# The second block's norm totals in a two-block transformer kernel: from 16 matmuls over feature tiles to two sums on VectorE and four matmuls

## The chip, the cores and the metric

The kernel runs on one core of one Trainium2 chip. The metric is the device time of one execution in microseconds (us).

## The reference, cut to what matters

Two transformer blocks run one after the other on 256 tokens of 1024 features, in float32. The first ends with a norm of its own, and the second begins with a norm, so two stand in a row:

```python
def rmsnorm(x, g):
    y = x * rsqrt(mean(x * x, axis=-1) + EPS)
    return y * g
x1 = rmsnorm(x0, norm_final_g)       # end of the first block
hn = rmsnorm(x1, attn_norm_g_2)      # start of the second
proj = hn @ w_in_2                   # split into xc, b_gate, c_gate, q, k, v
```

Behind it come a short convolution, differential attention, a projection, and a mixture of 32 experts, whose weights (96 units of 2 MB) are all read from memory.

Both norms need one number a token. The first needs the total of x0 squared over the features. The second needs the mean of x1 squared, which is the first's factor squared times the total of (x0 g) squared. So the kernel makes two totals from x0, a plain one and one weighted by g squared, and the products of both norms are applied later: `proj` is computed from x0 times the two gains, and the factors of the tokens (`rstd`, `r12`) come in where q, k and v are normed or copied out.

## The kernel before, in words

**Layout.** The residual `xT` is stored with features on the 128 partitions, in KD = 8 feature tiles of 256 tokens. Every dense matmul is made in three: weights and activations are split into a high part (rounded to fp32r) and a low part (the rest), and high x high, low x high and high x low are summed. The weights of an item (`q2`, `k2`, `v2`, ...) come in four chunks of two feature tiles. ScalarE writes the high part of a chunk (`split`, L570 to L580), VectorE subtracts to get the low part (`split`, L1647 to L1654), TensorE multiplies (`chunk`, L1002 to L1033). There are four buffers for chunks; ScalarE's split of a chunk waits until TensorE has used the chunk four before it. A chunk of q2 or k2 is 12 matmuls of 512 columns.

**Order.** Each engine's program is written out by hand, and so is the order of work. Semaphores join them. SP issues the loads in the order of a list; a load waits until the last item in its slot was split by VectorE (L448) and, for experts, until the unit ten before it was used by TensorE (L479).

**The edited stage** begins when the first block's last residual is there, tile after tile.

- ScalarE (L803 to L814): for each of the 8 tiles it writes the high part of the input and a square of `xT` into `n_sq` (`norm_square`, L588 to L594); then it splits q2's chunks 2 and 3, all of k2, two chunks of v2; then it waits for the spreads (`norm_bc` at 4), copies the second one out (L812), squares q2 (L814) and splits the rest of v2.
- TensorE (L1313 to L1326): q2's chunks 0 to 2; the totals (`norm_totals`, L1077 to L1086: for each tile and each half of the tokens one matmul of 128 x 128 squares with the two columns of `gain_sq`, 1 and g squared, into PSUM); q2's chunk 3; k2's chunks 0 and 1; two spreads (`norm_spread`, L1088 to L1094), which put `rstd` and `r12_sq` of each token into every partition; k2's chunks 2 and 3; then v2, which waits for q2 to be copied out.
- VectorE (L2066 to L2133): low parts of the input, splits of q2's last two chunks and k2's first; the wait for the totals (`norm_sum` at 3) and the mean; one split of k2; then a chain of small steps with POOL, which computes the powers (L535, L544), to `r12_sq` (L2081); copies of q2 (L2086); k2's last two splits; the wait for the spreads; eight scalings of `xT` (L2092); the sum of q2's squares (L2109); v2's four splits.

`gain_sq` is filled at the start by VectorE (L1717, L1722). `n_t` is the second half of `wb`, `n_sq` the first; `wc` is scratch space.

Of the kernel before, what the change touches and what calls it, by code (L numbers as in the profile page):

```python
# [15 lines left out]
P = 128  # L16
# [177 lines left out]
def build(nc, t, out):  # L194
# [8 lines left out]
    def S(name):  # L203
        if name not in sems:
            sems[name] = ctx.enter_context(nc.semaphore(name))
        return sems[name]

    def sb(name, shape, dt=F32):
        return ctx.enter_context(nc.sbuf_tensor(name, shape, dt))

    with ctx:
# [34 lines left out]
        scale_m = sb("scale_m", [P, KD])  # L246
        scale_f = sb("scale_f", [P, KD])
        scale_2 = sb("scale_2", [P, KD])
        gain_sq = sb("gain_sq", [P, KD, 2])
        r12 = sb("r12", [P, TT])  # L250
        r12_sq = sb("r12_sq", [P, TT])
        eps_r = sb("eps_r", [P, TT])
# [36 lines left out]
        n_sq = wb[:, 0:KD * SEQ].rearrange("p (k n) -> p k n", k=KD)  # L289
        n_t = wb[:, KD * SEQ:2 * KD * SEQ].rearrange("p (k n) -> p k n", k=KD)  # L290
        n_row = wc[:, 1152:1152 + SEQ]
        CKQ = Q_RANK + KV_RANK + ROPE
        cqkv = wc[:, 0:TT * CKQ].rearrange("p (t n) -> p t n", t=TT)
        fqT = wa[:, 0:1024].rearrange("p (m n) -> p m n", m=4)
# [267 lines left out]
        def _(act):  # L562
# [7 lines left out]
            def split(name, a=0, b=None):  # L570

                it = IT[name]
                for ci in range(a, len(it["chunks"]) if b is None else b):
                    c = it["c0"] + ci
                    if ci == 0:
                        act.wait_ge(S(f"slot{it['slot']}_loaded"), it["loaded"])
                    if c >= CHUNKS:
                        act.wait_ge(S("chunk_used"), c - CHUNKS + 1)
                    src, n = raw_chunk(it, ci)
                    nc.scalar.activation(wh[:, c % CHUNKS, 0:n], src, ACT.Copy).then_inc(S("chunk_high"), 1)  # L580
# [225 lines left out]
                nc.scalar.activation(hH[:, k, :], xT[:, k, :], ACT.Copy, scale=scale_2[:, k:k + 1]).then_inc(S("norm_high"), 1)  # L806
                norm_square(2, k, XT_BASE[2] + k + 1)
            split("q2", 2)
            split("k2")
            split("v2", 0, 2)  # L810
            act.wait_ge(S("norm_bc"), 4)
            nc.scalar.activation(r12_sq_b, ps[:, 5, 0:SEQ], ACT.Copy).then_inc(S("r12_out"), 1)  # L812
# [185 lines left out]
        def _(pe):  # L998
            def mm(o_, l, r, start, stop):
                return nc.tensor.matmul(o_, l, r, start=start, stop=stop, skip_group_check=True)  # L1000
# [70 lines left out]
            def ada_turn(n):  # L1071
# [2 lines left out]
                    ins = nc.tensor.transpose(ps[:, 6, s * P:s * P + P], ada_row[:, s * P:s * P + P], ident[:])  # L1074
                ins.then_inc(S("ada_turned"), 1)

            def norm_totals(n, bank, k0=0, k1=KD):  # L1077

                rows_n = 2 if n == 2 else 1
                for k in range(k0, k1):  # L1080
                    pe.wait_ge(S("norm_sq"), SQ_BASE[n] + k + 1)
                    for tt in range(TT):
                        ins = mm(ps[:, bank, rows_n * tt:rows_n * tt + rows_n], n_sq[:, k, tt * P:tt * P + P],
                                 gain_sq[:, k, :] if n == 2 else ones[:, 0:1], k == 0 and tt == 0, k == KD - 1)
                if k1 == KD:
                    ins.then_inc(S("norm_sum"), 1)  # L1086

            def norm_spread(ready, count, src, bank, c0=0):  # L1088

                pe.wait_ge(S(ready), count)  # L1090
                for tt in range(TT):
                    ins = mm(ps[:, bank, c0 + tt * P:c0 + tt * P + P], src[:, tt:tt + 1].to_broadcast([P, P]), ident[:],
                             c0 == 0 and tt == 0, True)
                ins.then_inc(S("norm_bc"), 1)  # L1094
# [219 lines left out]
            chunk("q2", 0, hH, hL, True, ready=in_2)  # L1314
            chunk("q2", 1, hH, hL, True, ready=in_2)
            chunk("q2", 2, hH, hL, True, ready=in_2)
            norm_totals(2, 6)
            chunk("q2", 3, hH, hL, True, ready=in_2)
            chunk("k2", 0, hH, hL, True)
            chunk("k2", 1, hH, hL, True)  # L1320
            norm_spread("norm_rstd", 3, rstd, 7)
            norm_spread("norm_r12", 1, r12_sq, 5)
            chunk("k2", 2, hH, hL, True)
            chunk("k2", 3, hH, hL, True)
            pe.wait_ge(S("q2_out"), 2)
            linear("v2", hH, hL, True)  # L1326
# [311 lines left out]
        def _(dve):  # L1638
# [21 lines left out]
            def mean_sq(dst, src, width, sem):  # L1660
                V.tensor_scalar(dst, src, 1.0 / width, EPS, ALU.mult, ALU.add).then_inc(S(sem), 1)

            def norm_mean(n, count, bank):

                rows_n = 2 if n == 2 else 1
                dve.wait_ge(S("norm_sum"), count)
                cols = ps[:, bank, 0:rows_n * TT].rearrange("p (t r) -> p r t", t=TT)
                mean_sq(ms[:, 0:TT], cols[:, 0, :], D, "norm_ms")
                return cols

            def norm_apply(n, bc, scale, shift, between=None):

# [37 lines left out]
            for part in two_pi_parts():  # L1710
# [3 lines left out]
            V.tensor_scalar(trig[:, 2], trig[:, 2], pi_lo, -pi_lo, ALU.min, ALU.max).then_inc(S("rope_steps"), 1)  # L1714
            link(V.tensor_tensor(scale_2[:], colT[:, ROW["fin_g"]:ROW["fin_g"] + KD], colT[:, ROW["attn_g2"]:ROW["attn_g2"] + KD],
                                 ALU.mult))
            V.memset(gain_sq[:, :, 0], 1.0)  # L1717

            V.tensor_tensor(wr, wr, colT[:, ROW["ffn_g2"]:ROW["ffn_g2"] + KD].unsqueeze(2).to_broadcast([P, KD, LG]),
                            ALU.mult).then_inc(S("router_scaled"), 1)  # L1720
            fg = colT[:, ROW["fin_g"]:ROW["fin_g"] + KD]
            V.tensor_tensor(gain_sq[:, :, 1], fg, fg, ALU.mult)  # L1722
            norm_mean(0, 1, 5)

            dve.wait_ge(S("rope_steps"), 3)
# [340 lines left out]
            low_2(KD - 1)  # L2066
            split("q2", 2)
            split("k2", 0, 1)
            dve.wait_ge(S("norm_sum"), 3)
            cols = ps[:, 6, 0:2 * TT].rearrange("p (t r) -> p r t", t=TT)  # L2070
            mean_sq(ms[:, 0:TT], cols[:, 0, :], D, "norm_ms")
            split("k2", 1, 2)
            dve.wait_ge(S("norm_rstd"), 3)
            link(V.tensor_tensor(ssq[:, 0:TT], cols[:, 1, :], rstd[:, 0:TT], ALU.mult))
            link(V.tensor_tensor(ssq[:, 0:TT], ssq[:, 0:TT], rstd[:, 0:TT], ALU.mult))
# [10 lines left out]
                    V.tensor_copy(dst[:, tt, :], ps[:, IT[name]["acc"] + tt, :]).then_inc(S(f"{name}_out"), 1)  # L2086

            tok_out("q2", q2)
            split("k2", 2)
            dve.wait_ge(S("norm_bc"), 4)  # L2090
            for k in range(KD):
                V.scalar_tensor_tensor(out=xT[:, k, :], in0=xT[:, k, :], scalar=colT[:, ROW["fin_g"] + k:ROW["fin_g"] + k + 1],  # L2092
# [343 lines left out]
```

## Time and profile before

| | |
|---|---|
| time, median of 3 runs | 996.44 us (994.03 to 997.14) |
| span of the profiled execution, its own time | 1000.3 us |
| TensorE busy | 953.0 us, 95% |
| VectorE busy | 464.1 us, 46% |
| ScalarE busy | 378.7 us, 38% |
| GpSimd busy | 28.4 us, 3% |
| read from memory | 307.31 MB, 308 GB/s over the span |
| the edited stage | about 424 to 456 us |

The page gives the profiled execution's span and no time beside it, so the span stands for its own time. Busy shares are averages over stages with different limits: in the first half of the span TensorE, VectorE and ScalarE work on dense items, in the second expert weights stream in. A record of TensorE is one pass; a matmul of float32 operands leaves two. A timeline merges records that are alike: "x32" is 32 of them, and the duration then runs from the first's start to the last's end. "[0.75 <-DVE wl L1654]" at the end of a line means that the engine sat idle for 0.75 us and that the named instruction ended the wait. Line 1000 is the helper through which all matmuls go.

### The profile page before, as it was taken

The page shows a single profiled execution, that of the slowest core. Times are in us where ns is not written, and L with a number is a line of the kernel's source. Part 1 is how long each engine was busy: PE and PEld are TensorE (multiplying, and loading weights), DVE is VectorE, ACT ScalarE, POOL GpSimd, SP SyncE. Part 2 cuts the span into 40 slices and gives each one's busy share as a digit, 9 for nine tenths or more (in the row PEclk, how much of TensorE's full clock was granted, in tenths as well). Part 3 has the DMA queues.
Part 4 walks back from the last instruction along what each step waited for, and adds up shares of the span by engine and source line. Part 5 has one row for each costly group of instructions (what it writes and reads, how often), then busy time and mean ns, then how long its engine had stood idle before and what let it go on. Part 6 is the DMA issues. An engine that isn't in the chain of part 4 may idle for free.

```text
span 1000.3 us, 15301 instructions
## 1 busy us (share of the span) xinstructions
PE 953.0 (95%) x6325; PEld 666.8 (67%) x6325; DVE 464.1 (46%) x860; ACT 378.7 (38%) x718; POOL 28.4 (3%) x60
## 2 busy tenths in 40 slices
PE   6899999998999999999999899999999999998987
PEld 4798777998999999988987434343434344332433
DVE  3697766686777477657874211212121212120113
ACT  2455546654665366455662412121212111110210
POOL 1000000000000000002120000000000000000000
PEclk9999999999999999999999899999999999999999
DMA  9967853724645553634757699999999999999996
GB/s 384 397 274 281 321 204 127 273 101 169 252 169 190 209 192 127 251 104 168 293 207 309 263 429 427 427 428 428 425 429 428 428 427 427 428 427 428 428 428 267
DMA packets 23398, 309.35 MB, mean 309 GB/s; under 512 B 2592, under 2 KB 3104, under 8 KB 4000
## 3 DMA queue, kind: packets, MB, share of 16 engines
q1 hardware_dynamic: 23184, 307.32, 75.5%
q8 instruction: 50, 0.82, 0.3%
q10 hardware_dynamic: 144, 1.05, 0.3%
q14 instruction: 20, 0.16, 0.0%
HBM read 307.31 MB, written 1.05 MB: 308 GB/s over the span
## 4 chain that ended last, share of the span: by engine, by line
PE 74%; DMA 16%; DVE 6%; issue 1%; ACT 1%; POOL 1%; DVEq 0%
PE ps L1000 72%; DMA ring<-experts 4%; DMA work<-experts 4%; DMA slot<-experts 4%; DMA ring<-dense 4%; DVE wl L1654 2%; PE ps L1210 1%; PE ps L1581 1%; DVE ring L1738 1%; DMA colT<-cols 1%; POOL rstd L535 0%; PE ps L1523 0%; DVE xT L2092 0%; DVE wb L1959 0%; DVE wb L2169 0%
## 5 line engine op out<-in xcount | busy, mean ns | idle before, releaser
L1000 PE MATMUL ps<-hH,wh 128*128 128x256 f32 x704 | 199.6, 284 | 3.4 <-DVE hL L1678 1.9
L1654 DVE TENSOR_TENSOR wl<-ring,wh 128x1024 fp32r<-128x1024 f32 (+1 forms) x136 | 163.6, 1214 | 77.5 <-ACT wh L580 77.2
L1000 PE MATMUL ps<-hL,wh 128*128 128x256 f32 x704 | 197.2, 280 | 0.0
L1000 PE MATMUL ps<-hH,wl 128*128 128x256 f32 x704 | 197.2, 280 | 0.0
L580 ACT ACTIVATE wh<-ring 128x1024 fp32r<-128x1024 f32 (+1 forms) x136 | 140.3, 1043 | 115.3 <-PE ps L1000 91.0
L1000 PEld LDWEIGHTS ps<-hH,wh 128*128 128x128 f32 x704 | 134.4, 191 | 5.6 <-issue 3.6
L1000 PEld LDWEIGHTS ps<-hL,wh 128*128 128x128 f32 x704 | 133.1, 189 | 0.0
L1000 PEld LDWEIGHTS ps<-hH,wl 128*128 128x128 f32 x704 | 132.9, 189 | 0.0
L2361 DVE SCALAR_TENSOR_TENSOR wc<-wc,w_slot,ps 128x512 f32<-128x512 f32 x16 | 12.0, 748 | 220.8 <-PE ps L1000 220.8
L1000 PE MATMUL ps<-aH,wh 128*128 128x256 f32 x304 | 85.9, 283 | 0.7 <-DVE wb L2213 0.7
L1000 PE MATMUL ps<-aH,wl 128*128 128x256 f32 x304 | 85.0, 280 | 0.0
L1000 PE MATMUL ps<-aL,wh 128*128 128x256 f32 x304 | 85.0, 280 | 0.0
L2354 DVE TENSOR_TENSOR eL<-ps,eH 128x512 fp32r<-128x512 f32 (+1 forms) x33 | 22.3, 675 | 134.1 <-ACT eH L983 73.9
L1000 PE MATMUL ps<-ring,xT 128*64 128x512 f32 x304 | 68.6, 593 | 2.3 <-DMA ring<-experts 2.3
L1000 PE MATMUL ps<-slot,xT 128*64 128x512 f32 x288 | 64.5, 595 | 3.6 <-DMA slot<-experts 3.6
L1000 PEld LDWEIGHTS ps<-aH,wh 128*128 128x128 f32 x304 | 57.8, 190 | 2.1 <-issue 1.2
L1000 PEld LDWEIGHTS ps<-aH,wl 128*128 128x128 f32 x304 | 57.2, 188 | 0.0
L1000 PEld LDWEIGHTS ps<-aL,wh 128*128 128x128 f32 x304 | 57.1, 188 | 0.0
L1000 PE MATMUL ps<-work,xT 128*64 128x512 f32 x224 | 50.4, 595 | 3.7 <-DMA work<-experts 3.7
L1000 PEld LDWEIGHTS ps<-ring,xT 128*64 128x64 f32 x304 | 21.5, 137 | 46.7 <-issue 41.4
L1000 PEld LDWEIGHTS ps<-slot,xT 128*64 128x64 f32 x288 | 20.1, 137 | 44.7 <-issue 37.1
L965 ACT ACTIVATE wc<-ps,w_slot 128x512 f32<-128x512 f32 x16 | 11.0, 688 | 91.8 <-PE ps L1000 91.8
(351 smaller groups left out, 1421.1 us busy)
## 6 DMA issues: line engine op xcount, KB each, us to landing
ring<-dense SPq DMA_DIRECT2D x39, 2048.0 KB, 8.5
ring<-experts SPq DMA_DIRECT2D x28, 2048.0 KB, 27.9
slot<-experts SPq DMA_DIRECT2D x28, 2048.0 KB, 28.9
work<-experts SPq DMA_DIRECT2D x20, 2048.0 KB, 28.3
early<-experts SPq DMA_DIRECT2D x10, 2048.0 KB, 26.6
wb<-experts SPq DMA_DIRECT2D x9, 2048.0 KB, 25.3
early<-dense SPq DMA_DIRECT2D x4, 2048.0 KB, 9.3
ring<-dense SPq DMA_DIRECT2D x4, 1024.0 KB, 4.7
```

Of the source, the lines that this page charges most:

```text
L580: nc.scalar.activation(wh[:, c % CHUNKS, 0:n], src, ACT.Copy).then_inc(S("chunk_high"), 1)
L965: nc.scalar.activation(sg, ps[:, 0, :], ACT.Silu, scale=w_slot[:, 1:2]).then_inc(S("e_silu"), 1)
L1000: return nc.tensor.matmul(o_, l, r, start=start, stop=stop, skip_group_check=True)
L1210: ins = nc.tensor.transpose(ps[:, 4, i * P:i * P + P], prob_of(a)[:, c0:c0 + P], ident[:])
L1581: ins = nc.tensor.transpose(ps[:, 2, f * P:f * P + P], eact[:, f * P:f * P + P], ident[:])
L1654: V.tensor_tensor(wl[:, c % CHUNKS, 0:n], src, wh[:, c % CHUNKS, 0:n].bitcast(F32), ALU.subtract)\
L1738: ins = V.scalar_tensor_tensor(out=w, in0=w, scalar=1.0, in1=c_rep[:], op0=ALU.mult, op1=ALU.mult, accum_out=adaT[:, col:col + 1])
L2354: V.tensor_tensor(eL[:, cs], ps[:, bank, 0:n], eH[:, cs].bitcast(F32), ALU.subtract).then_inc(S("e_low"), 1)
L2361: V.scalar_tensor_tensor(out=eact, in0=sg, scalar=w_slot[:, 0:1], in1=ps[:, 1, :], op0=ALU.mult, op1=ALU.mult)\
```

## The change

It alters how the two totals are made and where on each engine that is done.

- ScalarE, between its splits of k2's chunks 0 and 1, makes a second set of squares: `xT` times g, squared, into `n_t`.
- VectorE, behind its split of k2's chunk 0, sums each set over the 8 feature tiles into 256 numbers a partition (`n_sum`, in `wc`), then splits k2's chunk 1. The split of k2's chunk 2 moves ahead of the wait for POOL's first power.
- TensorE makes the totals with four matmuls (two halves of the tokens, two sets) against one column of ones, between k2's chunks 0 and 1 and not between q2's chunks 2 and 3. The two spreads move from ahead of k2's chunk 2 to ahead of its chunk 3.
- `gain_sq` and its two instructions go.

```diff
--- before.py
+++ after.py
@@ -246,7 +246,6 @@
         scale_m = sb("scale_m", [P, KD])
         scale_f = sb("scale_f", [P, KD])
         scale_2 = sb("scale_2", [P, KD])
-        gain_sq = sb("gain_sq", [P, KD, 2])
         r12 = sb("r12", [P, TT])
         r12_sq = sb("r12_sq", [P, TT])
         eps_r = sb("eps_r", [P, TT])
@@ -289,6 +288,7 @@
         n_sq = wb[:, 0:KD * SEQ].rearrange("p (k n) -> p k n", k=KD)
         n_t = wb[:, KD * SEQ:2 * KD * SEQ].rearrange("p (k n) -> p k n", k=KD)
         n_row = wc[:, 1152:1152 + SEQ]
+        n_sum = wc[:, 1152:1152 + 2 * SEQ].rearrange("p (r n) -> p r n", r=2)
         CKQ = Q_RANK + KV_RANK + ROPE
         cqkv = wc[:, 0:TT * CKQ].rearrange("p (t n) -> p t n", t=TT)
         fqT = wa[:, 0:1024].rearrange("p (m n) -> p m n", m=4)
@@ -806,7 +806,11 @@
                 nc.scalar.activation(hH[:, k, :], xT[:, k, :], ACT.Copy, scale=scale_2[:, k:k + 1]).then_inc(S("norm_high"), 1)
                 norm_square(2, k, XT_BASE[2] + k + 1)
             split("q2", 2)
-            split("k2")
+            split("k2", 0, 1)
+            for k in range(KD):
+                nc.scalar.activation(n_t[:, k, :], xT[:, k, :], ACT.Square,
+                                     scale=colT[:, ROW["fin_g"] + k:ROW["fin_g"] + k + 1]).then_inc(S("norm_sq"), 1)
+            split("k2", 1)
             split("v2", 0, 2)
             act.wait_ge(S("norm_bc"), 4)
             nc.scalar.activation(r12_sq_b, ps[:, 5, 0:SEQ], ACT.Copy).then_inc(S("r12_out"), 1)
@@ -1074,14 +1078,22 @@
                     ins = nc.tensor.transpose(ps[:, 6, s * P:s * P + P], ada_row[:, s * P:s * P + P], ident[:])
                 ins.then_inc(S("ada_turned"), 1)
 
+            def feature_totals(bank):
+
+                pe.wait_ge(S("norm_sum"), 4)
+                for tt in range(TT):
+                    for r in range(2):
+                        ins = mm(ps[:, bank, 2 * tt + r:2 * tt + r + 1], n_sum[:, r, tt * P:tt * P + P], ones[:, 0:1],
+                                 tt == 0 and r == 0, True)
+                ins.then_inc(S("norm_sum"), 1)
+
             def norm_totals(n, bank, k0=0, k1=KD):
 
-                rows_n = 2 if n == 2 else 1
                 for k in range(k0, k1):
                     pe.wait_ge(S("norm_sq"), SQ_BASE[n] + k + 1)
                     for tt in range(TT):
-                        ins = mm(ps[:, bank, rows_n * tt:rows_n * tt + rows_n], n_sq[:, k, tt * P:tt * P + P],
-                                 gain_sq[:, k, :] if n == 2 else ones[:, 0:1], k == 0 and tt == 0, k == KD - 1)
+                        ins = mm(ps[:, bank, tt:tt + 1], n_sq[:, k, tt * P:tt * P + P], ones[:, 0:1], k == 0 and tt == 0,
+                                 k == KD - 1)
                 if k1 == KD:
                     ins.then_inc(S("norm_sum"), 1)
 
@@ -1314,13 +1326,13 @@
             chunk("q2", 0, hH, hL, True, ready=in_2)
             chunk("q2", 1, hH, hL, True, ready=in_2)
             chunk("q2", 2, hH, hL, True, ready=in_2)
-            norm_totals(2, 6)
             chunk("q2", 3, hH, hL, True, ready=in_2)
             chunk("k2", 0, hH, hL, True)
+            feature_totals(6)
             chunk("k2", 1, hH, hL, True)
+            chunk("k2", 2, hH, hL, True)
             norm_spread("norm_rstd", 3, rstd, 7)
             norm_spread("norm_r12", 1, r12_sq, 5)
-            chunk("k2", 2, hH, hL, True)
             chunk("k2", 3, hH, hL, True)
             pe.wait_ge(S("q2_out"), 2)
             linear("v2", hH, hL, True)
@@ -1662,11 +1674,8 @@
 
             def norm_mean(n, count, bank):
 
-                rows_n = 2 if n == 2 else 1
                 dve.wait_ge(S("norm_sum"), count)
-                cols = ps[:, bank, 0:rows_n * TT].rearrange("p (t r) -> p r t", t=TT)
-                mean_sq(ms[:, 0:TT], cols[:, 0, :], D, "norm_ms")
-                return cols
+                mean_sq(ms[:, 0:TT], ps[:, bank, 0:TT], D, "norm_ms")
 
             def norm_apply(n, bc, scale, shift, between=None):
 
@@ -1714,12 +1723,8 @@
             V.tensor_scalar(trig[:, 2], trig[:, 2], pi_lo, -pi_lo, ALU.min, ALU.max).then_inc(S("rope_steps"), 1)
             link(V.tensor_tensor(scale_2[:], colT[:, ROW["fin_g"]:ROW["fin_g"] + KD], colT[:, ROW["attn_g2"]:ROW["attn_g2"] + KD],
                                  ALU.mult))
-            V.memset(gain_sq[:, :, 0], 1.0)
-
             V.tensor_tensor(wr, wr, colT[:, ROW["ffn_g2"]:ROW["ffn_g2"] + KD].unsqueeze(2).to_broadcast([P, KD, LG]),
                             ALU.mult).then_inc(S("router_scaled"), 1)
-            fg = colT[:, ROW["fin_g"]:ROW["fin_g"] + KD]
-            V.tensor_tensor(gain_sq[:, :, 1], fg, fg, ALU.mult)
             norm_mean(0, 1, 5)
 
             dve.wait_ge(S("rope_steps"), 3)
@@ -2066,10 +2071,19 @@
             low_2(KD - 1)
             split("q2", 2)
             split("k2", 0, 1)
-            dve.wait_ge(S("norm_sum"), 3)
+
+            def feature_sum(r, squares):
+                V.tensor_reduce(n_sum[:, r, :], squares.rearrange("p k n -> p n k"), AX_X, ALU.add).then_inc(S("norm_sum"), 1)
+
+            dve.wait_ge(S("norm_sq"), SQ_BASE[2] + KD)
+            feature_sum(0, n_sq)
+            dve.wait_ge(S("norm_sq"), SQ_BASE[2] + 2 * KD)
+            feature_sum(1, n_t)
+            split("k2", 1, 2)
+            dve.wait_ge(S("norm_sum"), 5)
             cols = ps[:, 6, 0:2 * TT].rearrange("p (t r) -> p r t", t=TT)
             mean_sq(ms[:, 0:TT], cols[:, 0, :], D, "norm_ms")
-            split("k2", 1, 2)
+            split("k2", 2, 3)
             dve.wait_ge(S("norm_rstd"), 3)
             link(V.tensor_tensor(ssq[:, 0:TT], cols[:, 1, :], rstd[:, 0:TT], ALU.mult))
             link(V.tensor_tensor(ssq[:, 0:TT], ssq[:, 0:TT], rstd[:, 0:TT], ALU.mult))
@@ -2086,7 +2100,7 @@
                     V.tensor_copy(dst[:, tt, :], ps[:, IT[name]["acc"] + tt, :]).then_inc(S(f"{name}_out"), 1)
 
             tok_out("q2", q2)
-            split("k2", 2)
+            split("k2", 3)
             dve.wait_ge(S("norm_bc"), 4)
             for k in range(KD):
                 V.scalar_tensor_tensor(out=xT[:, k, :], in0=xT[:, k, :], scalar=colT[:, ROW["fin_g"] + k:ROW["fin_g"] + k + 1],
```

## Rows read from the trace of the kernel before

**Rows 1.** The page: span, DMA and granted clock in 40 slices of 25 us.
```profile
span 1000.3 us, 15301 instructions
...
PEclk9999999999999999999999899999999999999999
DMA  9967853724645553634757699999999999999996
```

**Rows 2.** The chain that ended last: start, duration (us), what.
```profile
450.30 3.22 DVE xT L2092 x8
453.71 1.14 DVE ms L2109
...
455.25 1.14 DVE wl L1654
456.52 17.01 PE ps L1000 x98
...
825.31 37.81 DMA slot<-experts
```

**Rows 3.** Windows of 5 us: busy us of each engine, PEclk, DMA share, GB/s.
```profile
555.00:560.00 5.00, 5.00 (x27) 5.00 (x26) 0.80 (x6) 2.19 (x7) 0.59 (x1) 0.55 0.22 95
...
565.00:570.00 5.00, 5.00 (x26) 1.85 (x24) 0.00 (x0) 1.50 (x4) 0.00 (x0) 1.00 0.99 357
```

**Rows 4.** Timeline of SP's queue of transfers: start, duration, what, how many.
```profile
564.16 0.33 SPq L439 DMA_DIRECT2D early<-experts  x1
```

**Rows 5.** Timeline of TensorE from q2's chunk 2 to k2's chunk 2.
```profile
435.78 3.63 PE L1000 MATMUL ps<-gain_sq,wb 128*128 128x2 f32 x32
439.27 0.48 PE L1000 MATMUL ps<-wh,hH 128*128 128x512 f32 x1
...
443.70 0.39 PE L1000 MATMUL ps<-wh,hH 128*128 128x512 f32 x1
...
449.21 0.61 PE L1000 MATMUL ps<-ident,rstd 128*128 128x128 f32 x4
...
450.02 0.47 PE L1000 MATMUL ps<-wh,hH 128*128 128x512 f32 x1
```

**Rows 6.** Window of 5 us behind the thin matmuls, columns as in rows 3.
```profile
440.00:445.00 5.00, 5.00 (x16) 3.92 (x16) 2.81 (x9) 1.06 (x1) 1.99 (x2) 0.66 0.12 52
```

**Rows 7.** Source view, ScalarE: durations (ns) min/median/max, first and last start, form.
```profile
L884 ACT ACTIVATE wb<-wb,colT x4: 495/496/502, 496.7 to 497.9; 128x256 f32<-128x256 f32 x4
```

**Rows 8.** Timeline of ScalarE: its four splits behind the squares.
```profile
430.55 3.89 ACT L580 ACTIVATE wh<-ring 128x1024 fp32r<-128x1024 f32 x4
```

**Rows 9.** Source view of three reduces of VectorE, columns as in rows 7.
```profile
L2109 DVE TENSOR_REDUCE ms<-work x2: 1212/1213/1214, 453.6 to 464.5; 128x16 f32<-128x1024 f32 x2
...
L2277 DVE TENSOR_REDUCE wa<-wa x1: 286/286/286, 549.6 to 549.6; 128x16 f32<-128x128 f32 x1
...
L2278 DVE TENSOR_REDUCE wa<-wa x1: 370/370/370, 549.8 to 549.8; 128x16 f32<-128x128 f32 x1
```

**Rows 10.** Timeline of VectorE in the edited stage.
```profile
431.63 3.50 DVE L1654 TENSOR_TENSOR wl<-ring,wh 128x1024 fp32r<-128x1024 f32 x3 [0.78 <-ACT wh L580]
439.45 0.16 DVE L1661 TENSOR_SCALAR ms<-ps 128x2 f32<-128x2 f32 x1 [4.32 <-PE ps L1000]
...
442.89 0.16 DVE L2081 TENSOR_TENSOR r_sq<-r 128x2 f32<-128x2 f32 x1
443.90 1.29 DVE L2086 COPY wa<-ps 128x512 f32<-128x512 f32 x2 [0.85 <-PE ps L1000]
```

**Rows 11.** Timeline of TensorE in two earlier stages.
```profile
46.08 0.40 PE L1000 MATMUL ps<-wh,hH 128*128 128x296 f32 x1 [2.55 <-DVE wl L1654]
...
234.52 1.05 PE L1000 MATMUL ps<-tri_ones,wb 128*128 128x1 f32 x8 [0.24 <-ACT wb L594]
```

**Rows 12.** Window behind the wait at 46.08, columns as in rows 3.
```profile
47.52:50.93 3.41, 3.41 (x16) 3.41 (x15) 3.41 (x6) 0.00 (x0) 0.00 (x0) 0.50 0.98 312
```

**Rows 13.** Waits: who waited for whom: us in total, times, longest.
```profile
PEld ps L1000 <- DMA slot<-experts: 7.2, 4, 2.1
```

## The prediction, made before the changed kernel was run

> **What bounds the kernel now.** I read the page first, then the chain of waits, and only then the stage that is edited. The page's last half is one flat stretch: the DMA engines are at 99% in every slice from the 24th on, and the chain that ended last goes three times through a transfer of some 40 us, of which the one of 37.81 stands for all [rows 1, 2]. The end of this kernel is a stream of expert weights. The stream has a clear start: DMA is busy 0.22 of the time in 555 to 560 us and 0.99 in 565 to 570, because ten units fill the ring of buffers early and the eleventh (`early<-experts`, issued at 564.16) waits for the first unit to be used by TensorE [rows 3, 4]. After it come 86 units of 2.1 MB; at the 428 GB/s of these slices they take 86 x 2.1 / 0.428 = 421 us, so until about 986 us, and the rest is tail. So whatever moves the first use of an expert unit moves the end by as much, and nothing else in the front half counts.
>
> The edited stage lies 130 us before that point. The chain there runs on engines alone: TensorE, then VectorE's eight scalings of `xT` (3.22 us), its sum of q2's squares (1.14), its split of v2's first chunk (1.14), and from 456.52 TensorE for 17 us in one piece [rows 2]. The reader is to see that the stage does not end with TensorE's work before it but with VectorE's work behind `norm_bc` (the spread of the norm over all rows): the spreads end at 450.02, TensorE's two remaining chunks of k2 need 2 x 2.755 us more, to 455.5, and v2 starts only at 456.52 [rows 2, 5]. From `norm_bc` to v2's first matmul is a fixed 6.5 us.
>
> **The change, part by part.**
>
> *TensorE loses the old totals.* 16 matmuls (32 records, two passes each) run from 435.78 to 439.27: 3.49 us [rows 5]. They are thin, and behind them the granted clock falls: 0.66 on average in 440 to 445, that is some 3.4 us at 1.2 instead of 2.4 GHz [rows 6]. q2's chunk 3 takes 4.43 us, from 439.27 to 443.70, where the next two chunks take 2.755 each ((449.21 - 443.70) / 2) [rows 5]: another 1.67 us. With both gone, q2 chunk 3 starts at 435.78 and k2 chunk 0 ends at 435.78 + 2 x 2.755 = 441.29.
>
> *ScalarE gets eight weighted squares* ahead of k2's chunk 1. The nearest row is the 128x256 activation with a column as scale at L884, 0.496 us each, started every 0.4 us (496.7 to 497.9 for four) [rows 7]. Its four splits from 430.55 take 3.89 us, so three are out by 433.5 and the squares by 436.8 [rows 8]; the split of k2's chunk 1 follows to 437.9. ScalarE has no other work here; VectorE's second sum needs the squares only at 438.6. Cost nothing, covered by VectorE's first sum; uncovered it would be 3.3 us.
>
> *VectorE gets two sums over the feature tiles*, 2048 elements in and 256 out each. No row has that shape, and this is the price that decides. The one long reduce of the trace reads in order: 1024 elements in 1.213 us, and with 128 in order in 0.286 that is 0.15 us plus 1.04 ns an element: 2.28 us each. But the new ones read with a stride (`p k n -> p n k`). The trace has one pair that differs in just that: L2277 in order takes 0.286 us, L2278 over the transposed view 0.370, so 1.70 ns an element [rows 9]: 0.15 + 2048 x 1.70 = 3.63 us each. I take 3.63, since it is the row with a stride. Upper bound: the excess for the stride doubled (the new stride is 1 KB, that of L2278 is 32 bytes), 2.36 ns an element, 5.0 us each. Lower bound 2.28.
>
> The Trainium skill's "VectorE: DVE Perf Modes" (The perf-mode tier table, and Rules for kernel authors) gives a reduce the 1x rate and says "Consider restructuring" of one on the hot path. At the 0.96 GHz of its specifications the rule's 1x rate makes 2.1 us a sum, an estimate, which is my lower case; L2278 disagrees, 1.6 cycles an element. "SBUF — State Buffer" (Door 1) says that each access to a new 16-byte line pays a penalty; by that the 1 KB stride costs what the 32-byte one does, near 3.63, and no run here shows it yet.
>
> *Where the sums end.* VectorE's three splits end at 431.63 + 3.50 = 435.1 [rows 10]. Two sums: 442.3. The split of k2's chunk 1, moved behind them, is 1.15 more: 443.45. TensorE has arrived at 441.3 and waits. The four new matmuls are eight records; the same form cost 1.05 us in the first block's norm [rows 11], so 442.35 to 443.4. k2's chunk 1 starts at 443.5, and the next two-chunk stretch (chunk 2 now stands ahead of the spreads) ends at 449.0.
>
> *The scalar chain.* From the mean at 439.45 to the end of `r12_sq` at 442.89 + 0.16 it takes 3.6 us now [rows 10]; from 443.5 it ends at 447.1, inside k2's chunk 2, so the spreads don't wait for it. That is what moving them one chunk later buys. Behind it come q2's two copies (1.29 for both) and now one split in place of two: k2's chunk 3 is ready at 449.6, and TensorE asks for it at 449.8. SP's queue waits for that split before it loads `cg` into k2's slot: about 2 us later than before, and v2 and xc, 17 us of TensorE work and more, stand ahead of cg [rows 2], so the load stays hidden; bg, w2o and the expert units queue behind it on SP, each behind work of TensorE that moves as v2 does. POOL's two powers move along with the chain and nothing else is queued behind them before q2's sum.
>
> *The spreads* take 0.81 (449.21 to 450.02) [rows 5]: now 449.0 to 449.8. Shift of `norm_bc`: 449.8 - 450.0 = -0.2 us. The fixed 6.5 us follow, so v2 starts at 456.3. Of the 4.1 us that TensorE gains (3.49 + 1.67 - 1.05), 2.2 go into waiting for the sums and most of the rest moves into the wait ahead of v2, since k2's chunk 3 comes after the spreads: it ends at 452.6, and TensorE now stands 3.7 us where it stood 1.0.
>
> *What the longer stand costs.* In the start-up part TensorE waited 2.55 us for a split, and 1.4 us after it resumed the clock stood at 0.50 for 3.4 us [rows 11, 12]. The waits of 2.1 us for expert weights lowered nothing [rows 1, 13]. A stand of 3.7 us is past the first: I expect the lower clock in v2, all TensorE work on the chain, and price it as above, 1.6 us. "TensorE: Matmul & The Clock Gate" of the Trainium skill (What's actually happening) says that idleness brings the gate back to half; by it the dip is only moved from q2 to v2, and the trace agrees as far as its rows go.
>
> *Small things.* The two `gain_sq` instructions at the start (L1717, L1722) stood ahead of VectorE's wait for TensorE's first totals (L1666), which covers them; uncovered they are under 0.3 us.
>
> **Sum.** -0.2 + 1.6 = +1.4 us. The profiled execution's span is 1000.3 [rows 1], nothing around it is given; the median of the runs shown is 996.44, 0.4% less, and I carry the difference over: 997.8. About 0.3%, 3 us, is what a measurement can tell from no change.
>
> **The rivals.** (a) *Cheap sums or a clock that holds.* With 2.28 us a sum all is ready when TensorE arrives at 441.3; the totals end at 442.35, the spreads at 442.35 + 5.5 + 0.8 = 448.65: -1.4, and +0.2 with the dip in v2. 995.0 to 996.6. For it: the row of 1.213 us. Against: L2278. Chance 0.2. (b) *Slower: VectorE's sums hold up TensorE long enough to lower its clock a second time.* Place: the wait before `feature_totals`. At 3.63 us a sum TensorE does next to nothing from 441.3 to 443.5, about 2.1 us of waiting and thin records, as long as the waits that kept the clock and not far from the 2.55 that lost it [rows 11, 13]; a dip in k2 delays the spreads by 1.6: +3.0, 999.4. At 5.0 us a sum the totals start at 445.0 and the spreads end at 452.6: +2.5, and with both dips +5.7, 1002.1. It decides from about 3.85 us a sum, where the stretch is 2.55 long. Chance 0.22. (c) *The plain saving arrives*: -3.49 - 1.67 + 1.05 = -4.1, 992.3, faster by 0.4%. It would need VectorE's 6.5 us behind `norm_bc` to be no bound, and the chain says they are. Chance 0.05. (d) The removed work changes nothing that counts, because the first use of an expert unit is set by something outside the stage: 996.4. DMA was idle before 564 and the chain has no transfer between, so only 0.03. The forecast keeps 0.5.
>
> **How the numbers follow.** Faster by over 0.3%: (c), and a little of (a) by chance, 0.06. Slower: (b), 0.22. Within: 0.72. The range leaves out (c) and the far end of (b): from 994.8, just below (a), to 1000.2, past the second dip with a little longer sums.
>
> **What would show it.** In the changed profile: two reduces of 2048 elements at 3.6 us each; TensorE idle about a microsecond ahead of eight thin records, then again 3 to 4 us ahead of v2; the granted clock at 1.00 in q2's chunk 3 and at half within v2; the spreads ending within a microsecond of where they were against q2's first chunk; and the first expert issue after the pause later by 1 to 2 us. I am wrong if the sums take 2.3 or 5 us, if v2 runs at the full clock, or if the pause before the expert stream moves by another amount than v2's start.

## The result, and the profile after

The changed kernel takes 999.52 us (median of 7 runs, 997.48 to 1007.65), the kernel before 994.80 in the same series (7 runs, 994.03 to 997.14). The ratio is 1.0051, 95% interval 1.0026 to 1.0076: slower by about half a per cent, and clear of no change. A second series of 12 runs gave 998.69 against 995.88, 1.0028 (1.0000 to 1.0057). The times of every kernel here fall, but for a few between, into a lower and an upper group some 7 us apart; in the first series two of the changed kernel's runs were in the upper group (1005.72 and 1007.65) and none of the kernel before's, so I read the sizes from the profiles.

The two profiled executions seem to say the opposite, 996.7 us of span against 1000.3 [rows 1]. They can't be compared as wholes: between 200 and 427 us, in code that the change does not touch, the one of before lost 5.5 us (the last section says to what). So I measure the stage from a fixed point inside it, the first matmul of q2's chunk 2. In both kernels that matmul starts 0.05 us after VectorE's split of the chunk ends. The landmarks of before are these pieces of its chain and its timeline, with 449.21, 450.02 and 564.16 from [rows 4, 5]:

```profile
432.91 17.36 PE ps L1000 x88
```

```profile
473.39 1.07 PE L1335 MATMUL ps<-ident,work 128*128 128x128 f32 x8
```

```text
from the start of q2's chunk 2 (us)          before    after   difference
to the end of the spreads (k2's last chunk)   17.11    18.92      +1.81
to v2's first matmul                          23.61    25.42      +1.81
to the transposes of q                        40.48    43.67      +3.19
to the first expert load after the pause     131.25   133.46      +2.21
```

The last two rows of the changed kernel are read from these lines:

```profile
470.75 1.07 PE L1347 MATMUL ps<-ident,work 128*128 128x128 f32 x8
```

```profile
560.54 0.33 SPq L439 DMA_DIRECT2D early<-experts  x1
```

The page of the changed kernel, its lines for span, clock and DMA. The plateau of the last half and the pause before it are as before:

```profile
span 996.7 us, 15261 instructions
...
PEclk9999999997999999999999899999999999999999
DMA  9967853724645544634758699999999999999996
```

The chain that ended last, in the stage. VectorE's sums and the split behind them now stand on it, where before had one piece of TensorE, from 432.91 to the spreads:

```profile
429.30 7.51 DVE wc L2076 x2
436.81 1.14 DVE wl L1666
437.99 8.26 PE ps L1004 x32
446.28 3.23 DVE xT L2106 x8
449.70 1.14 DVE ms L2123
451.23 1.14 DVE wl L1666
452.50 18.39 PE ps L1004 x98
```

TensorE's timeline (start, duration, line, what; idle time and releaser in brackets), against [rows 5]:

```profile
427.08 0.50 PE L1004 MATMUL ps<-wh,hH 128*128 128x512 f32 x1 [0.33 <-DVE wl L1666]
...
429.95 0.39 PE L1004 MATMUL ps<-wh,hH 128*128 128x512 f32 x1
...
432.70 0.39 PE L1004 MATMUL ps<-wh,hH 128*128 128x512 f32 x1
...
436.86 1.05 PE L1004 MATMUL ps<-tri_ones,wc 128*128 128x1 f32 x8 [1.25 <-DVE wc L2076]
437.99 0.50 PE L1004 MATMUL ps<-wh,hH 128*128 128x512 f32 x1
...
440.12 0.63 PE L1004 MATMUL ps<-wh,hL 128*128 128x512 f32 x1
...
442.25 0.58 PE L1004 MATMUL ps<-wh,hH 128*128 128x512 f32 x1
...
445.19 0.61 PE L1004 MATMUL ps<-ident,rstd 128*128 128x128 f32 x4
...
446.00 0.47 PE L1004 MATMUL ps<-wh,hH 128*128 128x512 f32 x1
...
452.50 0.47 PE L1004 MATMUL ps<-wh,hH 128*128 128x512 f32 x1 [3.50 <-DVE wl L1666]
```

Chunk 3 of q2 (from 429.95) takes 2.75 us where it took 4.43: the thin matmuls and the half clock behind them are gone. Then TensorE waits 1.25 us for the sums, runs the eight thin records, and the half clock (a granted clock of 0.50, 1.2 GHz) is back in k2's chunk 1: 0.63 us a matmul in place of 0.39, 4.26 for the chunk. It stands idle (its "stand" in what follows) for 3.50 us ahead of v2, and there the clock falls again. The windows show both stretches (columns as in rows 3):

```profile
438.00:443.00 5.00, 5.00 (x15) 4.01 (x16) 3.66 (x11) 0.51 (x1) 2.30 (x2) 0.66 0.00 0
452.00:457.00 5.00, 4.50 (x13) 3.61 (x14) 5.00 (x7) 0.00 (x0) 3.11 (x1) 0.66 0.22 43
```

VectorE's and ScalarE's new work in their timelines:

```profile
429.21 7.59 DVE L2076 TENSOR_REDUCE wc<-wb 128x256 f32<-128x2048 f32 x2
...
441.39 0.16 DVE L2095 TENSOR_TENSOR r_sq<-r 128x2 f32<-128x2 f32 x1
```

```profile
427.57 3.29 ACT L811 ACTIVATE wb<-xT,colT 128x256 f32<-128x256 f32 x8
```

The 1.81 us at the spreads add up. Gone: 3.49 of totals and 1.67 of slow clock. Added ahead of the spreads: 2.54 for the wait, the new totals and the hand-over (435.45 to 437.99), 2.75 for the chunk that now precedes the spreads, and 1.51 (4.26 - 2.75) of slow clock in chunk 1. 2.54 + 2.75 + 1.51 - 3.49 - 1.67 = 1.64. The other 0.17 is the slow clock's last matmul, the first of k2's chunk 2: that chunk takes 2.94 (442.25 to 445.19) in place of 2.75.

One thing the timelines show that was not tried: `r12_sq` is ready at 441.55 (441.39 + 0.16), and k2's chunk 1 ends at 442.25. Here the spreads could have stood ahead of k2's chunk 2, as before, without a wait. By these rows that would bring them forward by chunk 2, up to 2.9 us, an estimate.

### The profile page after: what moved, and what is told of

It is laid out like the page before. It is cut to its first block, busy times and chain, and to the rows that moved or that the text cites. A ratio compares the mean times of both kernels' runs of the same rounds, so it can differ in the third digit from the quotient of the medians.

```text
span 996.7 us, 15261 instructions
## 1 busy us (share of the span) xinstructions
PE 949.4 (95%) x6301; PEld 661.8 (66%) x6301; DVE 471.4 (47%) x860; ACT 380.9 (38%) x726; POOL 28.3 (3%) x60
## 4 chain that ended last, share of the span: by engine, by line
PE 71%; DMA 16%; DVE 8%; ACT 2%; issue 1%; POOL 1%; DVEq 0%
PE ps L1004 69%; DMA ring<-experts 4%; DMA work<-experts 4%; DMA slot<-experts 4%; DMA ring<-dense 3%; DVE wl L1666 3%; DVE wc L2076 1%; DVE ring L1743 1%; PE ps L1222 1%; PE ps L1593 1%; DMA colT<-cols 1%; ACT wh L580 1%; POOL rstd L535 0%; PE ps L1535 0%; ACT hH L806 0%
```

## The experiments

All kernels were timed beside the kernel before. The table gives the lengths from q2's chunk 2 as above, read in each kernel's profile. Up to v2 they repeat to 0.03 us in the four whose edits did not move v2 (25.42, 25.42, 25.39, 25.39), while the whole time moves by microseconds. The 11 us ahead of the transposes, from v2's chunk 2 on, take either 11.10 or 11.29 us, so differences of 0.2 there tell nothing.

```text
kernel                              to v2   to the trans-  to the first  whole time, ratio
                                            poses          expert load   to before (95%)
before                              23.61     40.48          131.25      1
changed                             25.42     43.67          133.46      1.0051 (1.0026 to 1.0076)
changed, again                      25.42     43.65          133.04      1.0028 (1.0000 to 1.0057)
changed, adds for the sums          22.08     41.78          131.96      0.9993 (0.9966 to 1.0020)
changed, early splits               21.59     38.19          128.24      0.9971 (0.9943 to 0.9999)
changed, stand filled               25.39     42.07          132.00      1.0015 (0.9987 to 1.0042)
changed, wait filled                23.89     42.35          132.15      1.0024 (0.9996 to 1.0052)
changed, no second squares          25.39     43.86          133.57      one run
changed, sums twice                 33.29     52.81          143.41      one run
before, order alone                 27.93     46.11          135.72      1.0048 (1.0019 to 1.0077)
before, early splits                22.68     39.27          128.96      0.9980 (0.9950 to 1.0009)
changed, adds and early splits      18.41     35.01          125.67      0.9983 (0.9950 to 1.0015)
the same, again                     18.42     35.02          125.31      0.9933 (0.9910 to 0.9957)
```

From the first expert load to the end of the span all 13 profiles take 436.0 to 436.3 us. What moves that load moves the end by as much.

**The changed kernel again**, as the control.

> The changed kernel once more, as the control for the other kernels of this series. Theory: the change costs what its stage shows, in three pieces: TensorE's wait of 1.3 us for VectorE's sums, and two stretches at half clock (in k2's chunk 1, in v2) that together cost 3 us, where the old kernel had one of 1.6. From the start of q2's chunk 2 to v2's start 25.4 us (before: 23.6), and to the first transposes of q 43.8 (before: 40.6); whole time 3 to 4 us above before. Rival: the measured 4.7 us come in part from elsewhere (the dense stretches ahead of the stage ran at a different pace in the two profiles, 5.5 us apart between 200 and 427 us, in code that is the same); then the stage shows 3.2 and the whole time differs from it by microseconds from run to run, either way.

25.42 and 43.65: the stage repeats. The whole time was 2.8 us above before here and 4.7 in the first series. The profiles carry less to the first expert load, 2.2 and 1.8 us. The second series' interval holds that; the first's begins at 2.6 us, and what it has beyond the profiles stays open.

**Adds of whole tiles in place of the strided reduces.**

```diff
-                V.tensor_reduce(n_sum[:, r, :], squares.rearrange("p k n -> p n k"), AX_X, ALU.add).then_inc(S("norm_sum"), 1)
+                link(V.tensor_tensor(squares[:, 0:4, :], squares[:, 0:4, :], squares[:, 4:8, :], ALU.add))
+                link(V.tensor_tensor(squares[:, 0:2, :], squares[:, 0:2, :], squares[:, 2:4, :], ALU.add))
+                V.tensor_tensor(n_sum[:, r, :], squares[:, 0, :], squares[:, 1, :], ALU.add).then_inc(S("norm_sum"), 1)
```

> The two strided reduces replaced by adds of whole tiles read in order (4 tiles, 2 tiles, 1 tile), on VectorE at the same place; about 2.4 us a set in place of 3.8. Theory: VectorE is done before TensorE gets there, so the wait of 1.3 us ahead of the four matmuls goes, and with so short a thin stretch k2's chunk 1 runs at the full clock: 3.0 us less than the changed kernel up to v2's start (22.4 in place of 25.4), the stretch at half clock in v2 stays. Whole time within 1 us of before. Rival: the stretch at half clock in k2 has nothing to do with the wait (the thin matmuls alone bring it); then only 1.3 us come back and chunk 1 still takes 4.3 us.

VectorE's timeline, and TensorE's:

```profile
428.48 1.22 DVE L2076 TENSOR_TENSOR wb<-wb 128x1024 f32<-128x1024 f32 x1
429.73 0.69 DVE L2077 TENSOR_TENSOR wb<-wb 128x512 f32<-128x512 f32 x1
430.46 0.43 DVE L2078 TENSOR_TENSOR wc<-wb 128x256 f32<-128x256 f32 x1
430.80 1.22 DVE L2076 TENSOR_TENSOR wb<-wb 128x1024 f32<-128x1024 f32 x1
```

```profile
434.71 0.95 PE L1004 MATMUL ps<-tri_ones,wc 128*128 128x1 f32 x8
435.52 0.48 PE L1004 MATMUL ps<-wh,hH 128*128 128x512 f32 x1
...
438.37 0.40 PE L1004 MATMUL ps<-wh,hH 128*128 128x512 f32 x1
```

A set takes 2.32 us (428.48 to 430.80), the wait is gone, and k2's chunk 1 takes 2.85. Up to v2 3.34 us came back (3.0 expected). The rival falls: the eight thin records alone (0.95 us) don't bring the half clock. Only 1.89 of the 3.34 reach the transposes, because the half clock in v2 grew: TensorE still stands 3.50 us ahead of v2, and v2 with xc's first half takes 19.7 us in place of 18.25. I had not expected that part.

**The wait ahead of the new matmuls filled.**

```diff
+                for _ in range(5):
+                    mm(ps[:, bank, 0:P], ones, ident[:], True, True)
                 pe.wait_ge(S("norm_sum"), 4)
```

> The changed kernel with five matmuls of ones by the identity (results not used), 1.1 us, in TensorE's wait ahead of the four new ones. Theory: the half clock in k2's chunk 1 follows that wait, so it goes and the totals come no later: v2 23.8 us after q2's chunk 2 in place of 25.4; the later one in v2 stays. Rival: the thin matmuls and the wait are too short together to matter and the half clock is drawn by something else: still 25.4.

TensorE's timeline:

```profile
442.33 1.28 PE L1004 MATMUL ps<-ident,tri_ones 128*128 128x128 f32 x10
443.78 1.05 PE L1004 MATMUL ps<-tri_ones,wc 128*128 128x1 f32 x8 [0.17 <-DVE wc L2078]
444.91 0.51 PE L1004 MATMUL ps<-wh,hH 128*128 128x512 f32 x1
...
447.79 0.39 PE L1004 MATMUL ps<-wh,hH 128*128 128x512 f32 x1
```

The sums are as late as in the changed kernel, only the idle time is gone, and chunk 1 takes 2.88 us: v2 after 23.89, 1.53 less. So of the 1.81 us that the stage lost up to v2, 1.5 are the clock. The wait is needed for it: without the wait (adds) or with the wait filled the clock stays up. Whether the wait would do it without the thin records behind it was not tried.

**TensorE's stand ahead of v2 filled.**

```diff
             chunk("k2", 3, hH, hL, True)
+            for _ in range(14):
+                mm(ps[:, 6, 0:P], ones, ident[:], True, True)
             pe.wait_ge(S("q2_out"), 2)
```

> The changed kernel with 14 matmuls of ones by the identity (results not used) between k2's chunk 3 and v2, about 3 us, within TensorE's stand. Theory: v2 starts at the same time, but at the full clock; 1.4 us less than the changed kernel to the transposes of q, v2's start unchanged at 25.4. Rival: the half clock in v2 follows the earlier wait and comes all the same; no gain. A second rival: the stand was not wholly idle time to fill, and v2 starts later by what the fill runs over.

v2 starts after 25.39 us, as in the changed kernel, and the transposes come at 42.07, 1.6 us earlier. The half clock in v2 is priced at that, and it comes from the stand.

**VectorE's first two splits of v2 ahead of its wait for the spreads.**

```diff
             split("k2", 3)
+            split("v2", 0, 2)
             dve.wait_ge(S("norm_bc"), 4)
...
             tok_sum("q2", HEAD2, 16)
-            split("v2")
+            split("v2", 2)
```

> The changed kernel with VectorE's splits of v2's chunks 0 and 1 moved ahead of its wait for the spreads; sums unchanged. Theory: TensorE's stand of 3.5 us ahead of v2 is VectorE's work behind the spreads (scalings, sum, split), so it goes, and with it the stretch at half clock in v2: 3.7 + 1.4 = 5 us less than the changed kernel, about 2 us below before. Rival: VectorE is then late with v2's chunk 2 or with the scalings, and the stand only moves into v2; gain under 2 us.

TensorE's timeline, from the thin records on:

```profile
436.13 1.20 PE L1004 MATMUL ps<-tri_ones,wc 128*128 128x1 f32 x8 [1.26 <-DVE wc L2076]
...
447.93 0.39 PE L1004 MATMUL ps<-wh,hH 128*128 128x512 f32 x1
...
464.53 1.07 PE L1347 MATMUL ps<-ident,work 128*128 128x128 f32 x8
```

v2 starts at 447.93 with no wait, 21.59 us in, and the transposes come at 38.19: 5.5 us below the changed kernel, 2.3 below before. The stand was VectorE's work behind the spreads, as the chain said. The whole time, 0.9971 (0.9943 to 0.9999), is just clear of no change.

**The same edit in the kernel before** (`split("v2", 0, 2)` behind `split("k2", 2)`).

> The kernel before with v2's first two splits ahead of VectorE's wait for the spreads, nothing else. Theory: its stand ahead of v2 is 1.0 us, so it gains 1.0 us (39.5 to the transposes in place of 40.5), a fifth of what the same edit gives the changed kernel. Rival: the edit is worth the same 5 us whatever the totals; then the change itself would be without merit in any order.

0.93 us to v2 and 1.2 to the transposes. The edit is worth 1.2 us where the stand is 1 us and 5.5 where it is 3.5 with a half clock behind it. The rival falls.

**Both edits in the changed kernel.**

> The changed kernel with both: the sums as adds of whole tiles, and v2's first two splits ahead of VectorE's wait for the spreads. Theory: both of TensorE's waits and both stretches at half clock go; from q2's chunk 2 to v2 18.3 us, to the transposes of q 35.2 (before 40.5, changed 43.7), so 5.2 us below before and 8.5 below the changed kernel: the plain saving of TensorE's work plus the old stand ahead of v2. Rival: with TensorE ahead of everything, VectorE (scalings, sum, splits, copies of k2) or POOL's power becomes the bound inside v2 or before the transposes, and only 3 us of the 5 arrive.

> The kernel with both edits (adds of whole tiles, early splits of v2) once more. Its profile was 5.5 us short of before at every landmark behind the stage, but its times lay on two levels, 4 at 990 to 992 and 8 at 995 to 998. Theory: the two levels are those of every kernel here (before: most near 995, many near 1001; the changed one: near 998 and 1005), set ahead of the stage by the pace of the dense matmuls between 240 and 430 us, 113.3 or 117.8 ns each, 1600 of them, 7 us; which one a run gets is chance, so the share of the upper level is nearer to a quarter this time, and a profile from the upper level would show the 117.8. Rival: without the stretches at half clock in the stage the slower pace lasts through the rest of the front half, or the new order itself brings the upper level; then two thirds of the runs are on it again.

TensorE's timeline in the first of the two profiles:

```profile
436.58 0.94 PE L1004 MATMUL ps<-tri_ones,wc 128*128 128x1 f32 x8
...
446.63 0.39 PE L1004 MATMUL ps<-wh,hH 128*128 128x512 f32 x1
...
463.23 1.07 PE L1347 MATMUL ps<-ident,work 128*128 128x128 f32 x8
```

No wait and no half clock from q2 to the transposes: 18.41 and 35.01 us, then 18.42 and 35.02, 5.5 below before and 8.7 below the changed kernel (5.2 and 8.5 expected). Against the kernel before with the same early splits it is 4.26 us shorter (39.27 - 35.01): with both waits gone, the 4.1 us that TensorE saves arrive. The whole time gave 0.9983 in the first series, with two thirds of its runs on an upper level about 7 us above the others, and 0.9933 (0.9910 to 0.9957) in the second, with one run of 12 clearly there and one between, 990.95 us against 995.60. Both profiles show the same stage, one from each level, so the level is not set in the stage. Why eight runs were on it in the first series and at most two in the second is open; the two series ran on different chips of the same kind, and the kernel before, timed beside each, had 5 of 29 and 4 of 23 runs above 1000 us. At either level this version is the shortest: 989 to 992 and 996 to 998, where the kernel before has most runs at 993 to 996 and the rest spread from 996.5 to 1005.5.

**The order alone**, in the kernel before: its 16 matmuls behind k2's chunk 0, the spreads ahead of k2's chunk 3.

```diff
-            norm_totals(2, 6)
             chunk("q2", 3, hH, hL, True, ready=in_2)
             chunk("k2", 0, hH, hL, True)
+            norm_totals(2, 6)
             chunk("k2", 1, hH, hL, True)
+            chunk("k2", 2, hH, hL, True)
             norm_spread("norm_rstd", 3, rstd, 7)
             norm_spread("norm_r12", 1, r12_sq, 5)
-            chunk("k2", 2, hH, hL, True)
             chunk("k2", 3, hH, hL, True)
```

(VectorE's splits of k2 move by one chunk each to fit.)

> The kernel before with its 16 matmuls moved to where the changed kernel has its four (behind k2's chunk 0) and the spreads ahead of k2's chunk 3; no second squares, no sums. Theory: the move alone delays the spreads by a chunk, 2.75 us, the thin matmuls still lower the clock once behind them, and the stand ahead of v2 grows to 3.7 us and lowers it a second time: v2 26.4 us after q2's chunk 2, the transposes at 44.6, 4 us above before. Rival: with the totals late but nothing to wait for, the stage is no longer than the changed kernel's, 43.7 or less, and the sums are to blame for all of it.

27.93 and 46.11: longer than expected, since the thin matmuls now ran into the half clock themselves (4.74 us for 32 records, 3.63 before) and k2's chunk 1 took 4.92. The rival falls: the move costs 4.3 us up to v2, and the new totals win 2.5 of them back.

```profile
435.10 4.74 PE L1000 MATMUL ps<-gain_sq,wb 128*128 128x2 f32 x32
439.70 0.77 PE L1000 MATMUL ps<-wh,hH 128*128 128x512 f32 x1
...
444.62 0.39 PE L1000 MATMUL ps<-wh,hH 128*128 128x512 f32 x1
...
454.67 0.77 PE L1000 MATMUL ps<-wh,hH 128*128 128x512 f32 x1 [3.48 <-DVE wl L1654]
```

**Each sum made twice.**

```diff
+                link(V.tensor_reduce(n_sum[:, r, :], squares.rearrange("p k n -> p n k"), AX_X, ALU.add))
                 V.tensor_reduce(n_sum[:, r, :], squares.rearrange("p k n -> p n k"), AX_X, ALU.add).then_inc(S("norm_sum"), 1)
```

> The changed kernel with each sum made twice. Theory: TensorE waits for the sums, so all of the added VectorE work is on the path: 7.6 us more to v2's start (33.0) and to the first expert issue, give or take one stretch at half clock. Rival: half of it is hidden because k2's chunk 0 covers it; it isn't, if TensorE waited already in the changed kernel.

```profile
429.68 3.89 DVE L2076 TENSOR_REDUCE wc<-wb 128x256 f32<-128x2048 f32 x1
433.60 3.78 DVE L2077 TENSOR_REDUCE wc<-wb 128x256 f32<-128x2048 f32 x1
437.30 3.58 DVE L2076 TENSOR_REDUCE wc<-wb 128x256 f32<-128x2048 f32 x1
440.91 3.59 DVE L2077 TENSOR_REDUCE wc<-wb 128x256 f32<-128x2048 f32 x1
```

v2 comes 7.87 us later: all of the added work is on the path. The four sums end 14.82 us after they start where the two took 7.59, 7.23 more; behind the longer wait (8.47 us) the thin records and the hand-over run at the half clock and take 0.59 more.

**No second squares.** ScalarE's eight instructions and VectorE's wait for them are left out, and the plain squares are summed twice, so the factor of the second norm is another one.

> The changed kernel without ScalarE's eight weighted squares; VectorE sums the plain squares twice, so the second factor is computed from the wrong total. Theory: the squares are covered by VectorE's first sum and cost nothing: 25.4 and 43.7 as before. Rival: they slow VectorE's sum of the same memory or delay the split of k2's chunk 1, and up to 3.3 us come back.

25.39 and 43.86: nothing comes back, and the two sums take 7.54 us in place of 7.59. The 0.19 more to the transposes is the piece of 11.29 in place of 11.10 us.

## Why the prediction was right, and where it was not

It named 997.8 us, 1.4 above before, and a range of 994.8 to 1000.2 that holds the 999.52. Part of that is luck. The 996.44 it started from was the median of three runs; that of seven is 994.80. As a difference from before the forecast was +1.4 with a range of -1.6 to +3.8, and the series gave +4.7 and +2.8. Whether the change is within 0.3%, to which 0.72 was given, the times don't settle: the intervals are 0.26% to 0.76% and 0.00% to 0.57%, and both hold 0.3%. The stage is 3.2 us longer at the transposes, and 2.2 and 1.8 us reach the expert stream. What came in the stage was rival (b) in its first form, +3.0 us, two stretches at half clock.

- *The removed totals*: 3.49 and 1.67 us gone, as said; chunk 3 of q2 takes 2.75.
- *ScalarE's squares*: 3.29 us for eight as priced, covered, shown by leaving them out.
- *The sums*: priced at 3.63 each by the one strided row, measured 3.80 (7.59 / 2). The lower bound by rows read in order, and the estimate from the 1x rate of the Trainium skill's "VectorE: DVE Perf Modes" (The perf-mode tier table), 2.1 us, are too low. The advice of the same page of the Trainium skill (Rules for kernel authors) on a reduce in the hot path, to restructure it, the trace bears out: adds of whole tiles take 2.32. The rule of the Trainium skill's "SBUF — State Buffer" (Door 1) on new 16-byte lines agrees: 1.78 ns an element at a stride of 1 KB, 1.70 at 32 bytes.
- *TensorE ahead of k2's chunk 1*: the wait, the totals and the hand-over, said 2.2 (441.3 to 443.5), measured 2.54; 1.25 of it is the wait. The prediction let rival (b) decide "from about 3.85 us a sum", where the stretch would be as long as the one stand that had lost the clock; the sums took 3.80. So the case lay at the edge that it had named, and it chose the other side.
- *Shift of the spreads*: said -0.2, measured +1.81. This is the step that failed: "Shift of `norm_bc`: 449.8 - 450.0 = -0.2 us" kept the full clock in k2's chunk 1. I had put the short wait beside the waits for expert weights, which kept the clock (four of 7.2 us in all, of which only the longest has the 2.1), and left the other case to rival (b) at 0.22. The wait of 1.25 us with thin records behind it lowered the clock in the changed kernel's two profiles, and in the three other kernels of the study that kept that wait as it was (early splits, stand filled, no second squares); filled, it did not. The filled wait gives the size, 1.53 us; the rest of the miss is mostly the longer sums. The sign "the spreads ending within a microsecond of where they were against q2's first chunk" failed by it: 22.88 us before (427.14 to 450.02), 24.91 after (421.09 to 446.00).
- *The stand ahead of v2*: said 3.7 and 1.6 for its clock; measured 3.50, and 1.65 for the clock (18.25 us from v2's start to the transposes, against 16.60 in the kernels that reach v2 without a wait); filling it gave 1.60 back. Against before it is only 1.38, since before itself needs 16.87 there, 0.19 of it in the piece of 11.29 us.
- *Carried to the end*: that the end moves as the first expert load does was right (436.0 to 436.3 us from it to the end in all profiles; the 421 us named for the 86 units should be 422). The load moved by 2.21 of the 3.19 us. The missing 0.98 lies in two pieces of TensorE's chain that the change does not touch: 0.46 in the one from 526.00 (20.51 us before, 20.05 after), where before ran at the slower of two paces (last section), and 0.47 in the one from 554.08 (14.01 before, 13.54 after), of which a half clock near 550 us covers less in the changed kernel (granted clock 0.81 and 0.84).

That the fixed 6.5 us of VectorE's work behind the spreads swallow what TensorE gains was the right reading: v2 came 6.50 us after the spreads (446.00 to 452.50), and moving two splits out of that chain freed it.

## What to carry to other kernels

A saving on one engine is worth what the next hand-over lets through. Here 4 us of TensorE time were saved and the releasing event came 1.8 us later, because the work that took its place on VectorE was the slow form (a reduce over a stride), and because the spreads were moved behind another chunk. Price a short wait of TensorE with the clock that it may cost behind it, and look first for work that can stand ahead of the wait: two splits moved, worth 1.2 us before the change, were worth 5.5 after it.

## What the runs showed of the hardware that I had not expected

**The dense matmuls have two paces at the full granted clock.** In the uninterrupted stretch of the first block's feed-forward part, a matmul of 256 columns starts every 113.3 ns in some profiles and every 117.8 in others, and it keeps its pace for some 180 us, until q2. The window from 300 to 400 us shows it (columns as in rows 3; the number behind the first busy time counts TensorE's matmuls), for the kernel before and then for the best kernel's two profiles:

```profile
300.00:400.00 100.00, 100.00 (x851) 100.00 (x851) 68.33 (x95) 53.64 (x69) 0.00 (x0) 1.00 0.49 179
```

```profile
300.00:400.00 100.00, 100.00 (x884) 100.00 (x884) 71.38 (x101) 56.03 (x74) 0.00 (x0) 1.00 0.50 183
```

```profile
300.00:400.00 100.00, 100.00 (x852) 100.00 (x851) 68.32 (x95) 53.59 (x69) 0.00 (x0) 1.00 0.49 179
```

The code in this stretch is the same in all kernels, and TensorE is busy throughout at a granted clock of 1.00. The stretch has 1584 such matmuls, so the two paces differ by 4.5 x 1584 = 7.1 us, about the distance between the two groups into which the times of all these kernels fall. Of the best kernel's profiles the one at the faster pace belongs to a run of 991.87 us, the other to one of 996.42. Three of the 13 profiles have the slower pace: before, the best kernel's second, and the filled-wait kernel's, from a run of 1004.03; the two whose time is known are from the upper group, and the faster profiles of kernels with several runs are all from the lower one. What sets the pace is open; within this stretch it didn't change in any profile. It is why the slower kernel had the shorter span, and why a change of 3 us needs the lengths of its own stage.

**A strided reduce is a little faster while the other engines stand.** With the sums made twice, the first two took 3.89 and 3.78 us, while ScalarE made its squares and splits, and the last two 3.58 and 3.59, when ScalarE and TensorE both were idle. ScalarE's squares are not the cause: without them the two sums take 7.54 us in place of 7.59. Which of the two engines' other work makes the difference was not tried.
